# Six product jobs of a two-layer model kernel moved to later steps of its recurrence block, and sixty-five constant products taken out

## The chip, the cores and the metric

The kernel runs on one core of one Trainium2 chip. The metric is device time in microseconds (us), the median over the runs shown. The core's engines are TensorE (PE in the profile; its weight loads are the rows PEld), VectorE (DVE), ScalarE (ACT), GpSimd (POOL) and SyncE (SP), which issues the loads. Each engine takes its own instructions in order, and the engines wait for each other on semaphores.

## The reference, cut to what matters

The model is a stack of two transformer layers with local, low-rank and grouped attention, and then a third layer of another kind. That one has a mixer with four branches (a gated linear recurrence, the gated delta rule, stick-breaking attention and gated linear attention), and a mixture of experts behind it. Sequence 256, model width 1024, all in float32. The change lies in the mixer, where the first two branches are computed:

```python
proj = jnp.einsum("bsd,de->bse", x, w_in)          # one wide input projection for all branches
(a_in, gdn_qkv, gdn_beta_in, gdn_decay_in, gdn_gate_in,
 sb_qkv, gla_qkv, gla_lr, gla_gate_in, merge_in) = jnp.split(proj, offsets, axis=-1)
y_a = rg_lru(a_in, ...)                            # conv, two gates, a scan over time
qkv = silu(causal_depthwise_conv(gdn_qkv, gdn_conv_w))
q = l2_normalize(q) * GDN_DK ** -0.5;  k = l2_normalize(k)
o_b = gated_delta_rule_chunked(q, k, v, g, beta)
y_b = rms_norm_2(o_b, gdn_norm_w) * silu(gdn_gate_in)

def gated_delta_rule_chunked(q, k, v, g, beta):    # chunks of 64, 4 heads of 128
    gc = jnp.cumsum(g, axis=-1)
    decay = jnp.exp(jnp.where(causal, gc[..., :, None] - gc[..., None, :], -jnp.inf))
    a_mat = jnp.where(strict, (k_beta @ k^T) * decay, 0.0)
    t_inv = triangular_solve(a_mat, eye, unit_diagonal=True)
    u = t_inv @ (v * beta);  w = t_inv @ (k_beta * exp(gc))
    attn = (q @ k^T) * decay
    # scan over the 4 chunks:
    v_new = u_i - w_i @ state
    o_i = q_i @ state + attn_i @ v_new
    state = state * gl_i + kd_i^T @ v_new
```

## The kernel before, in words

Every float32 product with a large weight is made of three products of rounded halves. A weight unit of 128 x 2048 numbers (1 MB) is loaded, ACT rounds it to its high half (`Ring.hi`, L166 to L176), DVE subtracts to get the low half (`Ring.lo`, L179 to L188), and TensorE multiplies high by high, high by low and low by high (`products`, L472). The ring of this part holds four raw units and two split pairs: the high half of a unit waits until the unit two before it has been multiplied (`used`), and SyncE issues the load of a unit when the unit four before it has been split (`feed`).

`lru_and_gdn` (L2973) computes the first two branches. They are a chain of small operations that depend on each other, so the rest of the input projection is woven in: 44 jobs, numbered 0 to 43 here, two of them to a unit. Each is 24 products of 128 x 256, ended by one copy out of the bank by ACT (L618, L2823 with silu for jobs 20 to 23, or L2833), into banks 6 and 7 in turn, so a job waits until the job two before it has been copied out. `woven` (L2740) sets the order of all engines from the list `jobs_at`, which says how many jobs follow each of the 44 steps (0 to 43) of the chain. For each step,

- TensorE does its part of the chain's step, then that step's jobs;
- ACT rounds units up to the one after that of the last job so far, then does its part of the chain, then copies the step's jobs out;
- DVE does its part of the chain, then splits units up to the same one.

```python
def unit_after(step, end):
    return split_after.get(step, ring.ahead(beside.jobs[end - 1].unit, 1) if end else first)
```

So the place of a job in the list sets three queues: TensorE's, where ACT rounds the unit ahead and copies out, and where DVE splits.

The chain's steps that matter here: 10, convolution and scan (L3309); 12, squares of q and k (L3315, L3316) behind ACT's silu (L3177, step 11); 13, their sums on TensorE (L3059), then Ln and Exp on ACT (L3184, L3187); 14, q and k scaled (L3321); 15 and 16, the spread decay (L3323, L3324) and its sums on TensorE (L3064, L3065 and sixteen at L3035); 17, the product of k with k (`kks`); 18, of k with q (`qks`), and the masks (L3338 to L3341); 19, the masked products (L3345, L3348); 20, the transpose of one of them (`turns`, L3041) and six mask operations (L3350 to L3357); 21 to 30, five rounds that double the blocks of the triangular inverse (L3035 on TensorE, L3147 on ACT, L3362 to L3372 on DVE); 31, k and v transposed and scaled (L3378, L3210); 32, the products `w_sum` and `uu_sum`; 33 to 40, the scan over four chunks, two steps each (L3119, L3391, L3125 to L3131, L3397); 41 and 42, the output norm (L3147, L3404, L3140, L3224, L3225, L3408).

Where TensorE would wait, the kernel has constant products: `keep_busy` (L266) multiplies the identity by a table of constants into a bank that is free, and nobody reads it. `Beside.keep_busy` (L601) takes the bank that the next job will use. One such product is two MATMUL records in the profile.

Of the kernel before, what the change touches and what calls it, by code (L numbers as in the profile page):

```python
# [229 lines left out]
def program(nc, A, OUT):  # L230
    es = ExitStack()
    with es:
# [2507 lines left out]
        def woven(ring, beside, jobs_at, chains, split_after=()):  # L2740


            ends = list(itertools.accumulate(jobs_at))
            split_after = dict(split_after)
            assert ends[-1] == len(beside.jobs)
            first, last = beside.jobs[0].unit, beside.jobs[-1].unit

            def unit_after(step, end):
                return split_after.get(step, ring.ahead(beside.jobs[end - 1].unit, 1) if end else first)

            with nc.Block() as block:
                @block.sync
                def _(sp):
                    ring.feed(sp, ring.ahead(last, 1))

                @block.tensor
                def _(pe):
                    chain = chains["tensor"](pe)
                    for n in jobs_at:
                        next(chain, None)  # L2760
                        beside.multiply(pe, n)
                    for _ in chain:
                        pass

                @block.scalar
                def _(act):
                    chain = chains["scalar"](act)
                    for step, end in enumerate(ends):
                        ring.hi(act, unit_after(step, end))
                        next(chain, None)  # L2770
                        beside.leave(act, True, end)
                    for _ in chain:
                        pass

                @block.vector
                def _(dve):
                    chain = chains["vector"](dve)
                    for step, end in enumerate(ends):
                        next(chain, None)
                        ring.lo(dve, unit_after(step, end))  # L2780
                        beside.leave(dve, False, end)
                    for _ in chain:
                        pass


        def mixer(ring, s1, U_A, U_QKV, U_GGATE, U_MERGE, U_SB, U_GLA, U_LGATE, U_BR, U_OUT, load_rows):
# [50 lines left out]
            with ExitStack() as s2:  # L2837
# [51 lines left out]
                def small_products(pe):  # L2889
# [3 lines left out]
                    for t in range(TILES):  # L2893
# [3 lines left out]
                        for c in range(KD if t == 0 else 0):  # L2897
# [10 lines left out]
                jobs += fm_jobs(U_GGATE, yT[1], 0, ACT.Silu) + fm_jobs(U_SB[1], sk, all_act=True) + tok_jobs(U_SB[2], sv)  # L2908
                jobs += fm_jobs(U_GLA[0], q, all_act=True) + fm_jobs(U_GLA[1], k, all_act=True) + tok_jobs(U_GLA[2], vt)
                lru_and_gdn(ring, Beside("rec", ring, jobs, (6, 7)), ain, qkv, work, par, w_ax, tok8, hrow, eps_col,  # L2910
                            yT[0], yT[1], (CONV_A, CONV_B, B_A, B_X, LAM, CONV_G, GDN_N))

# [60 lines left out]
        def lru_and_gdn(ring, beside, ain, qkv, work, par, w_ax, tok8, hrow, eps_col, y_lru, y_gdn, columns):  # L2973
# [3 lines left out]
            def W(i):  # L2977
                return work[i]
# [7 lines left out]
            def half(flat, b):  # L2986
                return flat[:, 512 * b:512 * b + 512]
# [10 lines left out]
            with ExitStack() as st:  # L2998
# [27 lines left out]
                def tensor(pe):  # L3026
# [6 lines left out]
                    def eights(banks, left, right, sem):  # L3033
                        for g in range(8):
                            ins = nc.tensor.matmul(ps[banks[g // 4]][:, (g % 4) * P:(g % 4 + 1) * P], left(g), right(g),  # L3035
                                                   start=True, stop=True)
                        ins.then_inc(sem, 1)
# [6 lines left out]
                    def of(i):  # L3044
                        return lambda g: g8(W(i))[:, g, :]
# [31 lines left out]
                    eights((0, 1), lambda g: g8(kT)[:, g, :], lambda g: g8(qT)[:, g, :], qks)  # L3077
                    yield
                    yield
                    beside.keep_busy(pe, 11)  # L3080
                    pe.wait_ge(attn.sem, 2)
                    turns((2, 3), W(AT), an_turned)
                    yield
                    for n in range(5):
                        if n == 0:
                            beside.keep_busy(pe, 31)
                            pe.wait_ge(started.sem, 4)
                            pe.wait_ge(attn.sem, 4)
                        else:
                            pe.wait_ge(u_ready.sem, 2 * n)  # L3090
                        pe.wait_ge(mid_ready.sem, n + 1)
                        eights((0, 1), of(AM), of(U), y_sum)
                        yield
                        pe.wait_ge(y_out.sem, 2 * n + 2)
                        if n:
                            pe.wait_ge(t_ready.sem, 2 * n)
                        eights((2, 3), of(TN), of(Y), u_sum)
                        if n < 4:
                            eights((4, 5), of(Y), of(TN), t_sum)
                        yield  # L3100
# [2 lines left out]
                    turns((0, 1), kT, kv_turned)  # L3103
                    turns((2, 3), vT, kv_turned)
                    yield
                    beside.keep_busy(pe, 8)
                    pe.wait_ge(keyed.sem, 4)
                    eights((4, 5), of(KBE), of(U), w_sum)
                    pe.wait_ge(v_out.sem, 8)
# [23 lines left out]
                        ins.then_inc(o_sum, 1)  # L3133
                        yield
                    yield
                    beside.keep_busy(pe, 7)
                    pe.wait_ge(squared.sem, 3)
                    pe.wait_ge(u_out.sem, 2)
                    for b in range(2):
                        nc.tensor.matmul(ps[b][:, :], ones, half(W(SQ), b), start=True, stop=True).then_inc(n_sum, 1)  # L3140
                    beside.keep_busy(pe, 14)
                    yield

                def scalar(act):
# [263 lines left out]
                    done(dve, v.tensor_tensor(y, y, W(RS), ALU.mult), normed)  # L3408
                    yield

                jobs_at = [2] * 15 + [1, 1, 2, 1, 1] + [0] + [0, 1] * 4 + [0, 0] + [0, 0] + [1, 0] * 4 + [0] * 3
                woven(ring, beside, jobs_at, {"tensor": tensor, "scalar": scalar, "vector": vector})


# [331 lines left out]
```

## Time and profile before

| | us |
|---|---|
| runs shown: median of 3 | 1769.69 |
| lowest and highest | 1764.97, 1770.83 |
| profiled execution, its own time | 1771.72 |
| its span in the trace | 1770.0 |
| PE, DVE, ACT busy over the span | 1646.3, 1222.2, 818.0 |
| mean granted TensorE clock | 0.974 of full speed |

The span is from the first to the last instruction; the rest of the profiled execution's time lies around it. A granted clock of 1.00 is TensorE's upper level, 2.4 GHz, and 0.5 is the lower, 1.2 GHz. Busy time of TensorE counts a MATMUL as busy until its modelled end, so neighbouring rows overlap; the start times tell the pace. The recurrence block lies from about 978 us to 1217 us of the span.

### The profile page before, as it was taken

To read this page: it belongs to the slowest core of one execution; us is meant where nothing else is said; L and a number is where in the kernel's file an instruction comes from. 1 tells how busy PE (TensorE), PEld (TensorE's weight loads), DVE (VectorE), ACT (ScalarE), POOL (GpSimd) and SP (SyncE) were. 2 spreads that over 40 slices of the span, in tenths; PEclk is the share of its full clock that TensorE was granted. 3 is DMA by queue.
4 is the path that set the end of the run, shared out by engine and by line. 5 is a ranking of instruction groups with operands and counts; after the bars stand their busy time and mean duration, and the time that the engine had idled before them with its cause. 6 is when DMAs were issued, how large, how long until landed. Compare 5 with 4: busy or idle time off the path is not lost. (4 is left out here: it accounts for less than half of the span.)

```text
span 1770.0 us, 26752 instructions
## 1 busy us (share of the span) xinstructions
PE 1646.3 (93%) x11331; PEld 1501.3 (85%) x11331; DVE 1222.2 (69%) x1352; ACT 818.0 (46%) x952; POOL 42.9 (2%) x60
## 2 busy tenths in 40 slices
PE   3899998899999999899989899898899999999995
PEld 3889888899898988899979899888888787888884
DVE  5877577888766648756555785633574868899895
ACT  2345543333344554444433465224452347777774
POOL 0100000000010000000000000000000000000000
PEclk9999999999999999999999999998997999999998
DMA  8974435999855324566626564111222447999993
GB/s 306 328 237 151 159 119 159 346 321 323 288 165 153 120 96 128 196 211 215 225 76 192 158 185 126 52 45 48 72 96 72 143 144 249 387 357 367 363 360 127
DMA packets 226061, 348.13 MB, mean 197 GB/s; under 512 B 14612, under 2 KB 156672, under 8 KB 225808
## 3 DMA queue, kind: packets, MB, share of 16 engines
q1 hardware_dynamic: 225936, 346.36, 58.6%
q8 instruction: 91, 1.49, 0.3%
q14 instruction: 34, 0.28, 0.0%
HBM read 345.29 MB, written 1.97 MB: 196 GB/s over the span
## 5 line engine op out<-in xcount | busy, mean ns | idle before, releaser
L472 PE MATMUL bank<-layer_split,hT_pair 128*128 128x256 f32 (+2 forms) x4032 | 515.4, 288 | 19.0 <-DVE hT_pair L1056 7.8
L472 PEld LDWEIGHTS bank<-layer_split,hT_pair 128*128 128x128 f32 x4032 | 488.6, 191 | 32.8 <-issue 15.6
L188 DVE TENSOR_TENSOR layer_split<-layer_raw,layer_split 128x2048 fp32r<-128x2048 f32 x122 | 279.6, 2292 | 100.2 <-ACT layer_split L176 98.7
L176 ACT ACTIVATE layer_split<-layer_raw 128x2048 fp32r<-128x2048 f32 x122 | 233.6, 1915 | 193.8 <-PE bank L472 76.3
L188 DVE TENSOR_TENSOR expert_split<-expert_raw,expert_split 128x2048 fp32r<-128x2048 f32 x96 | 219.0, 2288 | 26.4 <-ACT expert_split L176 26.0
L176 ACT ACTIVATE expert_split<-expert_raw 128x2048 fp32r<-128x2048 f32 x96 | 183.4, 1917 | 55.8 <-PE bank L2515 31.4
L472 PE MATMUL bank<-split_w,hT_pair 128*128 128x256 f32 (+1 forms) x1248 | 175.2, 303 | 12.0 <-ACT mixer_arena L2833 3.6
L472 PEld LDWEIGHTS bank<-split_w,hT_pair 128*128 128x128 f32 x1248 | 164.1, 202 | 22.3 <-issue 12.7
L1931 PE MATMUL bank<-layer_split,ffnh_aT 128*128 128x512 f32 x528 | 127.0, 396 | 2.8 <-DVE ffnh_aT L2005 2.8
L188 DVE TENSOR_TENSOR split_w<-raw_w,split_w 128x2048 fp32r<-128x2048 f32 x39 | 89.4, 2292 | 45.6 <-ACT split_w L176 45.2
L472 PE MATMUL bank<-hT_pair,split_w 128*128 128x256 f32 x960 | 118.5, 283 | 2.0 <-DVE hT_pair L326 1.2
L1931 PEld LDWEIGHTS bank<-layer_split,ffnh_aT 128*128 128x128 f32 x528 | 98.0, 188 | 25.8 <-DVE ffnh_aT L2005 3.3
L472 PEld LDWEIGHTS bank<-hT_pair,split_w 128*128 128x128 f32 x960 | 115.4, 190 | 4.0 <-DVE hT_pair L326 1.8
L176 ACT ACTIVATE split_w<-raw_w 128x2048 fp32r<-128x2048 f32 x39 | 74.6, 1912 | 37.8 <-PE bank L472 33.7
L2515 PE MATMUL bank<-expert_split,hT_pair 128*128 128x512 f32 x384 | 90.4, 392 | 0.9 <-ACT gathered_pair L2626 0.9
L2515 PE MATMUL bank<-expert_split,gathered_pair 128*128 128x512 f32 x384 | 90.7, 392 | 0.0
L266 PE MATMUL bank<-cst 128*128 128x128 f32 x630 | 81.5, 289 | 4.2 <-PEq L3715 4.2
L2515 PEld LDWEIGHTS bank<-expert_split,hT_pair 128*128 128x128 f32 x384 | 71.5, 188 | 16.1 <-ACT gathered_pair L2626 1.3
L2515 PEld LDWEIGHTS bank<-expert_split,gathered_pair 128*128 128x128 f32 x384 | 71.5, 188 | 14.8
L266 PEld LDWEIGHTS bank<-cst 128*128 128x128 f32 x630 | 78.2, 203 | 5.4 <-issue 5.1
L1972 ACT ACTIVATE ffnh_aT<-bank 128x512 fp32r<-128x512 f32 x22 | 13.1, 597 | 85.9 <-PE bank L1919 85.9
L208 DVE SCALAR_TENSOR_TENSOR ada_acc<-layer_raw,silu_c,ada_acc 128x1024 f32<-128x1024 f32 x40 | 51.4, 1285 | 1.4
(470 smaller groups left out, 1966.4 us busy)
## 6 DMA issues: line engine op xcount, KB each, us to landing
layer_raw<-in_ada_w SPq DMA_DIRECT2D x48, 1024.0 KB, 7.1
layer_raw<-in_ffn_w_gate_up SPq DMA_DIRECT2D x44, 1024.0 KB, 6.1
layer_raw<-in_w_in SPq DMA_DIRECT2D x38, 1024.0 KB, 6.6
expert_raw<-in_w_gate SPq DMA_DIRECT2D x32, 1024.0 KB, 7.5
expert_raw<-in_w_up SPq DMA_DIRECT2D x32, 1024.0 KB, 7.5
expert_raw<-in_w_down SPq DMA_DIRECT2D x32, 1024.0 KB, 7.4
raw_w<-in_w_in SPq DMA_DIRECT2D x30, 1024.0 KB, 5.5
layer_raw<-in_ffn_w_down SPq DMA_DIRECT2D x22, 1024.0 KB, 5.6
```

The source lines that it names most:

```text
L176: self.nc.scalar.activation(self.pair[:, j % self.pairs, 0, 0:self.size[n]], self.raw[n % self.depth][:, 0:self.size[n]], ACT.Copy).then_i ...
L188: self.nc.vector.tensor_tensor(self.pair[:, j % self.pairs, 1, 0:self.size[n]], self.raw[n % self.depth][:, 0:self.size[n]], self.pair[:, ...
L208: self.nc.vector.scalar_tensor_tensor(acc[:, :], second, self.scale[:, 2 * q + 1:2 * q + 2], acc[:, :], ALU.mult, ALU.add).then_inc(self.l ...
L266: nc.tensor.matmul(ps[bank][:, 0:P], ident, cst[:, 0:P], start=True, stop=True)
L472: ins = nc.tensor.matmul(out, lhs, rhs, start=first and c == chunks[0] and tp + wp == 0, stop=last and c == chunks[-1] and tp == 1)
L1931: ins = nc.tensor.matmul(ps[4 + 2 * t + nb][:, :], self.aT[:, tp, c, t * P:(t + 1) * P], w[:, c, nb * 512:(nb + 1) * 512], start=n == 0 an ...
L1972: nc.scalar.activation(self.aT[:, 0, :, :].rearrange(flat), ps[2][:, :], ACT.Copy).then_inc(self.hi_out, 1)
L2515: ins = nc.tensor.matmul(ps[bank][:, :], gathered[e // PER // 2][:, tp, 4 * i + c, slot_cut(e // PER)], ring.view(u + i, wp, 4, 512)[:, c, :],
```

## The change

Nothing is computed otherwise. The list `jobs_at` has the same 44 steps and the same sum; jobs leave steps 10 to 14 (one of two in each) and step 16, and are put behind steps 19 (one more), 20 (two), 32, 41 and 42 (one each). By the cumulative count the step of every job from 21 on is another than before, steps 22 to 28 and 33 to 39 keep one job at every other step. Constant products: all 11 ahead of the transpose in step 20, 25 of 31 in step 21, all 8 in step 32, all 7 and all 14 in step 42 are taken out. The 6 left in step 21 and the 4 in step 31 stay.

```diff
@@ -3077,13 +3077,12 @@
                     yield
                     yield
-                    beside.keep_busy(pe, 11)
                     pe.wait_ge(attn.sem, 2)
                     turns((2, 3), W(AT), an_turned)
                     yield
                     for n in range(5):
                         if n == 0:
-                            beside.keep_busy(pe, 31)
+                            beside.keep_busy(pe, 6)
                             pe.wait_ge(started.sem, 4)
                             pe.wait_ge(attn.sem, 4)
@@ -3103,7 +3102,6 @@
                     turns((0, 1), kT, kv_turned)
                     turns((2, 3), vT, kv_turned)
                     yield
-                    beside.keep_busy(pe, 8)
                     pe.wait_ge(keyed.sem, 4)
                     eights((4, 5), of(KBE), of(U), w_sum)
@@ -3133,12 +3131,10 @@
                         yield
                     yield
-                    beside.keep_busy(pe, 7)
                     pe.wait_ge(squared.sem, 3)
                     pe.wait_ge(u_out.sem, 2)
                     for b in range(2):
                         nc.tensor.matmul(ps[b][:, :], ones, half(W(SQ), b), start=True, stop=True).then_inc(n_sum, 1)
-                    beside.keep_busy(pe, 14)
                     yield
@@ -3408,7 +3404,7 @@
-                jobs_at = [2] * 15 + [1, 1, 2, 1, 1] + [0] + [0, 1] * 4 + [0, 0] + [0, 0] + [1, 0] * 4 + [0] * 3
+                jobs_at = [2] * 10 + [1] * 5 + [1, 0, 2, 1, 2] + [2] + [0, 1] * 4 + [0, 0] + [0, 1] + [1, 0] * 4 + [1, 1, 0]
                 woven(ring, beside, jobs_at, {"tensor": tensor, "scalar": scalar, "vector": vector})
```

## Rows read from the trace of the kernel before

**Rows 1.** Stages of the block: busy us and count of each engine, granted clock, DMA share, GB/s.

```profile
1035.00:1065.00 30.00, 29.15 (x246) 28.64 (x245) 24.96 (x27) 19.11 (x21) 0.00 (x0) 1.00 0.57 176
1065.00:1083.50 18.50, 17.47 (x131) 15.38 (x129) 8.57 (x7) 14.43 (x16) 0.00 (x0) 1.00 0.52 158
...
1118.20:1163.60 45.40, 38.80 (x328) 37.66 (x328) 23.10 (x26) 10.56 (x16) 0.00 (x0) 1.00 0.16 47
...
1171.50:1206.40 34.90, 34.90 (x226) 30.72 (x224) 10.61 (x18) 6.22 (x8) 0.00 (x0) 0.90 0.20 61
1206.40:1217.30 10.90, 8.38 (x48) 7.15 (x47) 3.74 (x3) 6.08 (x7) 0.00 (x0) 0.82 0.00 0
```

**Rows 2.** Timeline, steps 9 to 18: start, length, engine, line, what, [idle before, releaser].

```profile
1042.06 23.06 PE L472 MATMUL bank<-hT_pair,split_w 128*128 128x256 f32 x192 [0.39 <-DVE split_w L188]
...
1050.23 1.28 ACT L2823 ACT_TABLE_LOAD   x1
1051.20 2.29 DVE L188 TENSOR_TENSOR split_w<-raw_w,split_w 128x2048 fp32r<-128x2048 f32 x1
1051.52 0.38 ACT L2823 ACTIVATE y_gdn<-bank 128x256 f32<-128x256 f32 x1
...
1055.76 2.94 ACT L3177 ACTIVATE mixer_arena<-mixer_arena 128x1024 f32<-128x1024 f32 x3
...
1058.74 1.23 DVE L3315 TENSOR_TENSOR mixer_arena<-mixer_arena 128x1024 f32<-128x1024 f32 x1 [0.55 <-ACT mixer_arena L3177]
...
1064.96 3.59 PE L3059 MATMUL bank<-mixer_arena,cst 128*128 128x512 f32 x8
...
1068.65 2.85 ACT L3184 ACTIVATE mixer_arena<-bank,eps_column 128x512 f32<-128x512 f32 x4
...
1072.81 2.00 ACT L3187 ACTIVATE mixer_arena<-mixer_arena 128x1024 f32<-128x1024 f32 x2
1073.90 2.49 DVE L3321 SCALAR_TENSOR_TENSOR mixer_arena<-mixer_arena 128x1024 f32<-128x1024 f32 x2 [4.24 <-ACT mixer_arena L3187]
...
1075.25 1.92 ACT L176 ACTIVATE split_w<-raw_w 128x2048 fp32r<-128x2048 f32 x1
...
1079.48 0.69 DVE L3323 COPY mixer_arena<-gdn_tok 128x1024 f32<-128x1024 f32 x1
...
1083.50 0.28 PE L3064 MATMUL bank<-gdn_tok,cst_second 128*128 128x8 f32 x2
...
1087.43 2.99 PE L472 MATMUL bank<-split_w,hT_pair 128*128 128x256 f32 x24
...
1097.70 1.95 PE L3035 MATMUL bank<-mixer_arena 128*128 128x128 f32 x16
```

**Rows 3.** Timeline, steps 19 to 21: the mask phase.

```profile
1107.63 1.40 DVE L3345 TENSOR_TENSOR mixer_arena<-mixer_arena,bank 128x512 f32<-128x512 f32 x2
...
1109.08 1.09 PE L3041 MATMUL bank<-cst,mixer_arena 128*128 128x128 f32 x8 [1.33 <-DVE mixer_arena L3345]
...
1110.01 7.09 PE L266 MATMUL bank<-cst 128*128 128x128 f32 x62
1110.50 1.22 DVE L3350 TENSOR_TENSOR mixer_arena<-mixer_arena,cst_second 128x1024 f32<-128x1024 f32 x1
...
1118.27 2.05 PE L3035 MATMUL bank<-mixer_arena 128*128 128x128 f32 x16 [1.17 <-DVE mixer_arena L3357]
```

**Rows 4.** Timeline, steps 32 and 33.

```profile
1167.77 3.84 PE L3035 MATMUL bank<-mixer_arena 128*128 128x128 f32 x32 [0.37 <-DVE mixer_arena L3378]
...
1171.54 1.09 PE L3119 MATMUL bank<-mixer_arena 128*64 128x128 f32 x8
```

**Rows 5.** Timeline, steps 41 and 42: the tail.

```profile
1206.47 3.35 PE L266 MATMUL bank<-cst 128*128 128x128 f32 x14
...
1210.83 0.69 ACT L3224 ACTIVATE mixer_arena<-bank,eps_column 128x512 f32<-128x512 f32 x1 [1.87 <-PE bank L3140]
...
1211.49 3.29 PE L266 MATMUL bank<-cst 128*128 128x128 f32 x28
```

## The prediction

> **What bounds the kernel now.** I read the page for the busy shares, then the table of stages of the block that is changed, then its timeline row by row. In the stages before the mask phase TensorE is busy 29.15 of 30.0 us and 17.47 of 18.5 us, with DVE at 24.96 and 8.57 [rows 1]. The reader should see the pace: eight jobs run without a break in 23.06 us, 2.88 us each [rows 2]. So TensorE sets the pace there, with DVE and ACT not far behind. In the mask phase it is the other way round: the 62 constant records stand inside DVE's six mask operations, and the next product waited for DVE, not for TensorE [rows 3]. In the inverse rounds one job a round lies on TensorE's path; that stays. The granted clock is 1.00 up to the inverse and falls to 0.90 and 0.82 in the scan and the tail [rows 1].
>
> **The change: 1. Six jobs leave steps 10 to 16.** If TensorE alone set the pace they would give 6 x 2.88 = 17.3 us. I follow the chain with one job a step. Jobs 18 to 22 end at 1042.06 + 5 x 2.88 = 1056.5. ACT has the silu table at 1050.23 + 1.28, copies job 20 out (0.38) and can start the silu (2.94 us) at 1051.9 instead of 1055.76, as the scan's operations and their split start at 1051.20 and the convolution is over before; it ends at 1054.9. The two squares (about 1.26 each from L3315's 1.23) end at 1057.4, and TensorE's sums (3.59 us) run from 1056.5 to 1060.1 [rows 2].
>
> ACT meanwhile rounds unit 12 (1.92), copies job 22 out and loads the table of Ln: ready at 1058.8. Ln 2.85, table 1.28, Exp 2.00 take it to 1065.0, and q and k are scaled at 1066.5 (L3321 ends 3.58 us after L3187 begins). Now comes something new: job 23 is a silu job and its copy lands behind the Exp. It needs the silu table again, 1.28 + 0.38 = 1066.6, and only then unit 13 is rounded (1068.5) and split (2.29: 1070.8), ahead of the spread decay on DVE (0.69: 1071.5). TensorE's L3064 starts at 1071.6 instead of 1083.50: 11.9 us earlier [rows 2]. TensorE has done jobs 24 and 25 by then, and waits some 2 us. From L3064 to the product of k with q it is 14.20 us before, with three jobs in it; two are left, one 2.88 less. Total of this part: **-14.8 us**. The Exp table has to come back too, in step 17, but there its result is asked for only after two more jobs, 5.8 us of TensorE. Bounds: -17.3 if nothing of ACT or DVE shows; -9.3 if one more round of table load, rounding and split (1.28 + 1.92 + 2.29 = 5.5) falls into the chain than I counted.
>
> What the chain of steps 10 to 16 is worth hangs on the table load. The row shows 1.28 us and the next activation 0.01 us behind it [rows 2]. The Trainium skill, "ScalarE: Activation LUTs", section "What ACT_TABLE_LOAD costs", gives about 1.28 us for the load and about 1.38 us more for a drain at each switch; with the drain at the three switches in the chain this part would be about 4 us smaller by an estimate from that page. The row shows no such drain, so the sum goes without it.
>
> **2. The mask phase.** Steps 19 and 20 get three jobs more (8.6 us of TensorE at 2.88), for 36 constant products of about 0.23 us (7.09 / 31), 8.2 us [rows 3]. That exchange is even and lies beside DVE's masks. But each engine's queue moves with the jobs. Step 18's split (now of unit 15, before of unit 18) stays where it was, in front of L3345. Unit 16 must now be split behind the masked products of step 19, ahead of L3350 on DVE's queue, and nothing stood between L3348 and L3350 before: 2.29 us on the path to the inverse's first product. ACT can round it in time, since job 29, which frees the pair, ends some 5 us before. Job 30 waits for unit 15's split, so TensorE stands idle some 2.5 us there, and the transpose starts about 1.6 us after its time of 1109.08; DVE needs it two masks after L3350, some 4 us later. Unit 17's split falls behind the last mask, beside the first product (2.05 us), and is hidden [rows 3]. **+2.3 us**; bounds 0, if ACT's wait covers it, and +4.6, if both splits show.
>
> **3. Inverse rounds.** One job in every second step as before. The splits move from rounds 1 and 3 to rounds 2 and 4, and DVE has 23.10 busy of 45.4 us there [rows 1]: nothing.
>
> **4. Step 32.** Eight constant products stood ahead of the wait for the scaled keys; they were free. The job 37 stands behind the 32 records of L3035, and the scan's first product L3119 started at 1171.54, 3.77 us after they started, right behind them [rows 4]. Everything in the scan hangs on that product, and each of its steps has a job as before. So the job's whole 2.9 us are on the path: **+2.9 us**. Bounds: 0, and +4.6 if it runs at the lower clock (below).
>
> **5. The tail.** Job 42 takes the place of the 7 constant products and of the rest of the wait for the squares: 1206.47 + 2.9 = 1209.4, just when the sums could start. But ACT now copies it out (0.38) before it loads the Ln table (1.28), which was loaded in idle time: L3224 starts at 1211.1 instead of 1210.83, say 0.4 with the hand-overs. And in this very place the 14 records took 3.35 us where 28 took 3.29 us later [rows 5]: lower clock, 1.2 GHz, behind the scan's short products. A job there loses 3.35 / 2 = 1.7 us. I take it: **+2.1 us**, bounds 0 and 2.1. Job 43 replaces the last 28 records (3.29 by 2.88) and hides behind Ln, Exp and the last product; unit 22's split moves behind the squares on DVE, where DVE waits for ACT's Ln and Exp in any case.
>
> **Loads.** SyncE's next loads follow the splits, some up to 20 us later than before. The DMA share is 0.57 and less [rows 1], and a unit is taken only every 3 to 10 us; four raw units stand ahead. No cost.
>
> **Sum**: -14.8 + 2.3 + 2.9 + 2.1 = **-7.5 us**. The profiled execution takes 1771.72 us, its span 1770.0; they would become 1764.2 and 1762.5. It stands 2.0 us above the median of the runs shown, 1769.69, so the median would be **1762.2 us**.
>
> **The rivals.**
>
> *The lead gives less.* ACT and DVE have 19.11 and 24.96 of 30 us [rows 1], and ACT's waits are taken away with the jobs. With the bound of -9.3 the sum is -2.0: 1767.7 us. Against it: the chain above counts each of their operations already. Chance 0.25.
>
> *The clock falls where the constant products went.* It is 0.90 in the scan [rows 1], and was at the lower level in the tail, right behind the scan's short products [rows 5]. In steps 31 and 32 only the transposes of k and v and the wait for the scaled keys are left between the inverse and L3035 x32. If it falls there, those 3.84 us [rows 4] lose up to 1.7 us: -5.8, 1763.9 us. Chance 0.12. In the mask phase a fall would be hidden: TensorE has some 3 us to spare. By the Trainium skill, "TensorE: Matmul & The Clock Gate", section "Part 4: PE-mode transpose", transposes do not count as activity for the clock, which speaks for this rival; rows 4 and 5 show no stretch of transposes with nothing else around them, so the trace is silent.
>
> *The lead gives nearly all.* The silu job's table load is hidden and the tail keeps the upper clock: -17.3 + 2.3 + 2.9 + 0.4 = -11.7, 1758.0 us. Chance 0.10.
>
> *Slower.* TensorE is busy in the lead only because its jobs fill a wait; what sets the end of step 16 is the chain silu, squares, Ln, Exp, scaling, spread on ACT and DVE, and its start hangs on the splits that DVE makes one behind the other. DVE's 24.96 of 30 us speaks for it. Then part 1 gives nothing and the added 2.3 + 2.9 + 2.1 = 7.3 stay: 1777.0 us. It decides from where part 1 gives under 2.0 us. Against it: the silu could have started 3.9 us earlier but for jobs 21 to 23 and their copies [rows 2], and TensorE's run of 23.06 us has no hole. Chance 0.08.
>
> **How the numbers follow.** The forecast, with 5.3 to 11 us saved, has 0.45. A difference under 0.3% (5.3 us) can't be told from none here: the three runs lie 5.9 us apart. Faster: 0.45 + 0.10 + half of the clock's 0.12 = 0.61. Within: 0.25 + 0.06 = 0.31. Slower: 0.08. The range goes from a little below the better case to just past the smaller lead, 1757 to 1769.5 us, and leaves the slower case out.
>
> **What would show it.** In the trace of the changed kernel: L3064 some 12 us and the product of k with q some 14 to 15 us earlier, and an added table load for L2823 and for L3193; a split L188 between L3348 and L3350, so that from L3345 to the inverse's first product 13 us pass and not 10.6; a job L472 x24 between L3035 x32 and the first L3119; job 42 from the end of the scan to the norm's sums, at 2.9 or 4.6 us. The forecast is wrong if the block's end comes less than 5 us earlier, or if the stages outside the block move.

## The result, and the profile after

The changed kernel takes **1757.51 us** (median of 10 runs, 1750.87 to 1762.47) against 1769.31 us for the kernel before in the same comparison (10 runs, 1762.95 to 1776.68): ratio 0.992, 95% interval 0.9903 to 0.9937, or 14.2 us less, with 11 to 17 in the interval (the ratio is taken over all runs; the medians themselves lie 11.8 us apart). The profiled execution takes 1758.45 us (span 1756.8) against 1771.72. Faster by more than 0.3% came true; the forecast of 1762.2 us took little over half of the gain. A second comparison (e10, below) gave 0.9935, and both together are about -12 us.

The totals of the page say little: TensorE's busy share stays at 93%.

```profile
span 1756.8 us, 26496 instructions
PE 1626.4 (93%) x11201; PEld 1483.1 (84%) x11201; DVE 1222.2 (70%) x1352; ACT 820.5 (47%) x954; POOL 46.5 (3%) x60
```

The stages of the block, in the changed kernel (columns as in [rows 1]):

```profile
1036.50:1066.50 30.00, 29.36 (x225) 26.93 (x224) 23.97 (x28) 24.17 (x27) 0.00 (x0) 1.00 0.57 176
1066.50:1072.60 6.10, 3.80 (x30) 3.39 (x29) 4.03 (x4) 4.97 (x6) 0.00 (x0) 1.00 0.01 3
1119.90:1159.60 39.70, 32.25 (x274) 31.06 (x272) 21.10 (x24) 11.51 (x22) 0.00 (x0) 1.00 0.18 54
1168.00:1203.00 35.00, 35.00 (x225) 30.77 (x225) 10.69 (x18) 7.32 (x8) 0.00 (x0) 0.90 0.20 61
1203.00:1213.90 10.90, 7.43 (x53) 6.27 (x52) 6.03 (x4) 6.74 (x9) 0.00 (x0) 1.00 0.31 96
```

ACT went from 19.11 to 24.17 us in the first 30, DVE stayed near 24, and then come 6.1 us in which TensorE has work for 3.80: at that point the pace has passed from TensorE to ACT and DVE. The tail kept the upper clock, 1.00 where it was 0.82.

Timeline of the lead in the changed kernel, from the sums of squares to the first products behind the spread decay:

```profile
1057.96 3.60 PE L3059 MATMUL bank<-mixer_arena,cst 128*128 128x512 f32 x8
...
1064.05 2.01 ACT L3183 ACTIVATE mixer_arena<-mixer_arena 128x1024 f32<-128x1024 f32 x2
1066.07 1.28 ACT L2823 ACT_TABLE_LOAD   x1
1067.37 0.38 ACT L2823 ACTIVATE y_gdn<-bank 128x256 f32<-128x256 f32 x1
1067.65 1.90 ACT L176 ACTIVATE split_w<-raw_w 128x2048 fp32r<-128x2048 f32 x1
1069.65 2.29 DVE L188 TENSOR_TENSOR split_w<-raw_w,split_w 128x2048 fp32r<-128x2048 f32 x1 [2.04 <-ACT split_w L176]
1071.86 0.69 DVE L3319 COPY mixer_arena<-gdn_tok 128x1024 f32<-128x1024 f32 x1
1072.60 0.39 PE L3064 MATMUL bank<-gdn_tok,cst_second 128*128 128x8 f32 x2 [1.70 <-DVE mixer_arena L3319]
```

Read down this list as one chain: Exp, the silu table loaded again for job 23, its copy, the rounding of a unit, its split, the spread, and only then TensorE. Six of the eight rows are ACT and DVE. The mask phase of the same kernel:

```profile
1095.73 1.40 DVE L3341 TENSOR_TENSOR mixer_arena<-mixer_arena,bank 128x512 f32<-128x512 f32 x2
1095.87 3.10 PE L472 MATMUL bank<-split_w,hT_pair 128*128 128x256 f32 x24 [2.66 <-DVE split_w L188]
1098.61 2.29 DVE L188 TENSOR_TENSOR split_w<-first_unit_raw,split_w 128x2048 fp32r<-128x2048 f32 x1
1100.82 1.22 DVE L3346 TENSOR_TENSOR mixer_arena<-mixer_arena,cst_second 128x1024 f32<-128x1024 f32 x1
...
1108.57 3.68 PE L3035 MATMUL bank<-mixer_arena 128*128 128x128 f32 x16 [1.94 <-DVE mixer_arena L3353]
```

A split of 2.29 us stands between the masked products and the next mask, where in [rows 3] nothing stood, and the job of step 19 waited 2.66 us for its split. Steps 31 to 33 and the tail of the same kernel:

```profile
1159.68 5.47 PE L3035 MATMUL bank<-mixer_arena 128*128 128x128 f32 x32 [2.16 <-DVE mixer_arena L3374]
1164.91 3.07 PE L472 MATMUL bank<-hT_pair,split_w 128*128 128x256 f32 x24
1167.91 1.09 PE L3117 MATMUL bank<-mixer_arena 128*64 128x128 f32 x8
...
1202.97 3.00 PE L472 MATMUL bank<-split_w,hT_pair 128*128 128x256 f32 x24
1206.41 1.28 ACT L3220 ACT_TABLE_LOAD   x1
1207.71 1.41 ACT L3220 ACTIVATE mixer_arena<-bank,eps_column 128x512 f32<-128x512 f32 x2
```

The job stands whole between the 32 records and the scan's first product. The records themselves took 5.47 us where [rows 4] has 3.84.

### The profile page after: what moved, and what is told of

The parts are those of the page before. It is cut to its first block and busy times, and to the rows that moved or that the text cites. A ratio compares the mean times of both kernels' runs of the same rounds, so it can differ in the third digit from the quotient of the medians.

```text
span 1756.8 us, 26496 instructions
## 1 busy us (share of the span) xinstructions
PE 1626.4 (93%) x11201; PEld 1483.1 (84%) x11201; DVE 1222.2 (70%) x1352; ACT 820.5 (47%) x954; POOL 46.5 (3%) x60
## 5 line engine op out<-in xcount | busy, mean ns | idle before, releaser
L472 PE MATMUL bank<-split_w,hT_pair 128*128 128x256 f32 (+1 forms) x1248 | 169.1, 296 | 13.3 <-PEq L513 3.5
L472 PEld LDWEIGHTS bank<-split_w,hT_pair 128*128 128x128 f32 x1248 | 158.1, 195 | 22.9 <-issue 11.4
L2515 PEld LDWEIGHTS bank<-expert_split,gathered_pair 128*128 128x128 f32 x384 | 71.5, 188 | 14.8
L266 PE MATMUL bank<-cst 128*128 128x128 f32 x500 | 67.1, 295 | 4.2 <-PEq L3711 4.2
L266 PEld LDWEIGHTS bank<-cst 128*128 128x128 f32 x500 | 64.4, 209 | 4.9 <-issue 4.7
```

The lines of the kernel that those rows point to most:

```text
L266: nc.tensor.matmul(ps[bank][:, 0:P], ident, cst[:, 0:P], start=True, stop=True)
L472: ins = nc.tensor.matmul(out, lhs, rhs, start=first and c == chunks[0] and tp + wp == 0, stop=last and c == chunks[-1] and tp == 1)
L2515: ins = nc.tensor.matmul(ps[bank][:, :], gathered[e // PER // 2][:, tp, 4 * i + c, slot_cut(e // PER)], ring.view(u + i, wp, 4, 512)[:, c, :],
```

## The experiments

Two questions stand behind them. Does each part of the change give what the forecast said, or did one (the lead above all) give more (e1 to e4, e6 to e8, e11, e12)? And is the rest of the gain the change's at all, or the comparison's, the clock's, or that of a mere shift of later stages (e5, e9, e10, e13 to e16)?

Line numbers in the diffs' kernels lie up to four below those of before. "Block" is the time from the table load of the first square root (1037.75 us in the kernel before; "after the square root" below counts from there too) to stick-breaking's first product, in one profile. The "lead" is the part up to the first masked product. Times are medians; "mean" is said where a mean is meant.

**e1: the lead and the mask phase in part.** Three jobs leave the lead, three enter steps 19 and 20.

```diff
-                    beside.keep_busy(pe, 11)
-                            beside.keep_busy(pe, 31)
+                            beside.keep_busy(pe, 6)
-jobs_at = [2] * 15 + [1, 1, 2, 1, 1] + [0] + [0, 1] * 4 + [0, 0] + [0, 0] + [1, 0] * 4 + [0] * 3
+jobs_at = [2] * 10 + [1] * 3 + [2] * 2 + [1, 1, 2, 1, 2] + [2] + [0, 1] * 4 + [0, 0] + [0, 0] + [1, 0] * 4 + [0] * 3
```

> Kernel before with three jobs taken from steps 10, 11, 12 and put behind steps 19 (one) and 20 (two), 36 constant products of the mask phase out, the rest (8, 7, 14) kept. Theory A (all gain is TensorE time taken from the lead, part by part, the clock is chance): three jobs give 3 x 2.88 = 8.6 us, the split between the masked products and the masks costs 2.2: -6.4 us, near 1763 us; from the first masked product to the first product of the inverse 12.8 us pass. Theory B (the change also acts on the stage of the gated linear attention, 100 us later, through the clock): 9 to 16 us saved, and that stage's scan is at the upper clock in this profile too.

1765.99 us (12 runs), ratio 0.9983 (0.9962 to 1.0003), before 1769.79. The timeline of the step behind the silu job:

```profile
1076.31 10.04 PE L472 MATMUL bank<-hT_pair,split_w 128*128 128x256 f32 x72 [8.41 <-ACT y_gdn L2823]
```

TensorE waited 8.41 us for the copy of job 23, which stands behind the Exp on ACT. The lead gave only 1.9 us for three jobs, and the mask phase cost its 2.2 us. Near 1763 us, 6.4 less, was expected; 3.8 less came, and the interval reaches from 0.9962 to past 1, so even that isn't clear. Which jobs leave matters as much as how many.

**e2: the other half.** Three jobs leave the lead, one goes to step 32 and two to the tail.

```diff
-                    beside.keep_busy(pe, 8)
-                    beside.keep_busy(pe, 7)
-                    beside.keep_busy(pe, 14)
-jobs_at = [2] * 15 + [1, 1, 2, 1, 1] + [0] + [0, 1] * 4 + [0, 0] + [0, 0] + [1, 0] * 4 + [0] * 3
+jobs_at = [2] * 13 + [1] * 2 + [1, 0, 2, 1, 1] + [0] + [0, 1] * 4 + [0, 0] + [0, 1] + [1, 0] * 4 + [1, 1, 0]
```

> Kernel before with three jobs taken from steps 13, 14, 16 and put behind steps 32, 41, 42, the constant products 8, 7, 14 out, those of the mask phase (11 and 31) kept. Theory A: 8.6 us from the lead, 2.9 given back in step 32, 0.4 in the tail: -5.3 us, near 1764 us; the first product of the scan starts 6.6 us behind the start of the 32 records before it at the upper clock, 8.2 at the lower one. Theory B: 8 to 15 us saved.

1760.02 us (8 runs), 0.9946 (0.9922 to 0.9969). The lead gave 12.0 us for three jobs, more than the 8.6 that they take on TensorE. The timeline of DVE shows where the rest comes from:

```profile
1083.80 2.29 DVE L188 TENSOR_TENSOR split_w<-first_unit_raw,split_w 128x2048 fp32r<-128x2048 f32 x1 [6.09 <-ACT split_w L176]
...
1089.36 1.23 DVE L3338 TENSOR_TENSOR mixer_arena<-mixer_arena,cst_second 128x1024 f32<-128x1024 f32 x1
1090.62 1.41 DVE L3342 TENSOR_TENSOR mixer_arena<-mixer_arena,bank 128x512 f32<-128x512 f32 x2
...
1093.50 2.29 DVE L188 TENSOR_TENSOR split_w<-raw_w,split_w 128x2048 fp32r<-128x2048 f32 x1
1095.71 1.22 DVE L3347 TENSOR_TENSOR mixer_arena<-mixer_arena,cst_second 128x1024 f32<-128x1024 f32 x1
```

A unit feeds two jobs, so its rounding and split fall in every second job. With an odd number of jobs ahead, step 18 has neither, and the masks of step 18 follow each other without a gap. But the split isn't gone: it stands behind the masked products now (1093.50), and from the first of them to the inverse's first product 12.85 us pass, where the kernel before has 10.64 with the same jobs and constants in that phase. So parity gave up to 3.4 us in the lead and took 2.2 back, about 1.2 us net. The whole time fell by 9.6 us where 5.3 were expected.

**e3: the job of step 32 in step 31**, ahead of L3035 x32 and beside DVE's last work on the inverse; otherwise the changed kernel.

```diff
-... + [0, 0] + [0, 1] + [1, 0] * 4 + [1, 1, 0]
+... + [0, 0] + [1, 0] + [1, 0] * 4 + [1, 1, 0]
```

> Changed kernel with the job of step 32 one step earlier, behind the transposes of k and v and ahead of the wait for the scaled keys. Theory A: the job runs in a wait of 2.4 us and costs 0.5 us where it cost 2.9: 2.4 us less than the changed kernel, and no low clock in the 32 records behind it (another 0 to 1.6): near 1754 us. Rival: the job was hidden in the wait for w and u behind step 32 already; then no difference.

1753.33 us (6 runs), 0.9918 (0.9889 to 0.9946).

```profile
1151.71 3.08 PE L472 MATMUL bank<-hT_pair,split_w 128*128 128x256 f32 x24
1154.63 3.73 PE L3035 MATMUL bank<-mixer_arena 128*128 128x128 f32 x32
1158.29 1.09 PE L3117 MATMUL bank<-mixer_arena 128*64 128x128 f32 x8
```

The scan's first product follows the 32 records directly again. From DVE's first L3364 in the inverse rounds (L3368 before) to it 48.17 us pass, 2.4 less than with the job in between at the upper clock (50.6): the price of step 32 is the job itself. Near 1754 us was expected.

**e4: the constants of step 32 back**, beside the job.

```diff
+                    beside.keep_busy(pe, 8)
                     pe.wait_ge(keyed.sem, 4)
```

> Changed kernel with the eight constant products ahead of the wait for the scaled keys put back. Theory A: they fill a wait and cost nothing; they keep the upper clock over the 32 records behind them, which took 5.47 us in the changed kernel and 3.84 in the kernel before: 0 to 1.6 us less than the changed kernel, mean 0.8. Rival (the low clock there is chance, not the missing products): the records can be at either clock here too, no difference on average.

1755.66 us (7 runs), 0.9927 (0.99 to 0.9954).

```profile
1156.68 1.95 PE L266 MATMUL bank<-cst 128*128 128x128 f32 x16
1159.01 3.84 PE L3035 MATMUL bank<-mixer_arena 128*128 128x128 f32 x32 [0.37 <-DVE mixer_arena L3375]
...
1165.60 1.09 PE L3118 MATMUL bank<-mixer_arena 128*64 128x128 f32 x8
```

The 32 records run at the upper clock, 3.84 us. Over all profiles without these constants and with the job behind the 32 records (the changed kernel twice, e2, e6, e7) they took 5.46 or 5.47 us in three and 3.84 in two. With something in the wait they never fell: 3.84 us in all eight profiles with the eight constants (this one and seven of kernels that kept them and have no job there), 3.73 in all five with a job there (e3, e8, e11, e12, e16). The Trainium skill, "TensorE: Matmul & The Clock Gate", section "Part 4: PE-mode transpose", has transposes not count as activity for the clock; the three falls of five, behind transposes and a wait of 2.16 us, agree with it. But the transposes stand in all eighteen profiles, so what these runs show is that the unfilled wait makes the difference, and not that transposes do.

**e5: the kernel before once more**, one run with a profile, no edit.

> The kernel before, a second profile. In the first one the stages behind the block (first stick-breaking product to the end) took 552.6 us, in the profiles of the changed kernel and the four variants 542.8 to 550.5. Theory A (where the clock falls there is chance): they take 543 to 552 us here too, and the block, from ACT's square root to the first stick-breaking product, 179.7 us again, give or take 1.7 us for a low stretch. Theory B (the change acts on the later stages): 552 us or more.

1767.03 us, span 1765.27. Its block takes 178.64 us against 179.66 in the profile ahead of the prediction, so that block repeats within 1.5 us (178.22 in e9), while its span is 4.7 us less. The difference lies in other stages.

**e6: the split held back.** Unit 13 (jobs 26 and 27) is rounded and split behind the spread decay on DVE, not ahead of it.

```diff
-woven(ring, beside, jobs_at, {"tensor": tensor, "scalar": scalar, "vector": vector})
+woven(ring, beside, jobs_at, {"tensor": tensor, "scalar": scalar, "vector": vector}, split_after={14: ring.ahead(beside.jobs[23].unit, 1)})
```

> Changed kernel, with the rounding and split of unit 13 held from step 14 to step 15, behind the spread decay. Theory: the chain of steps 10 to 16 hangs on ACT's two table loads and this split, not on TensorE: the spread decay starts right behind the scaling, about 4 us earlier, then TensorE's job 25 (which waits for the silu copy) is the last to come: L3064 1.8 us earlier than in the changed kernel (33.4 us behind the square root's start becomes 31.6), the whole time 1.8 us less. Rival (TensorE's jobs set the end of this part): no difference.

1754.52 us (6 runs), 0.9917 (0.9891 to 0.9942).

```profile
1064.41 0.69 DVE L3319 COPY mixer_arena<-gdn_tok 128x1024 f32<-128x1024 f32 x1
1064.56 3.09 PE L472 MATMUL bank<-hT_pair,split_w 128*128 128x256 f32 x24 [0.59 <-ACT y_gdn L2823]
...
1066.69 2.29 DVE L188 TENSOR_TENSOR split_w<-raw_w,split_w 128x2048 fp32r<-128x2048 f32 x1 [0.86 <-ACT split_w L176]
1067.49 0.28 PE L3064 MATMUL bank<-gdn_tok,cst_second 128*128 128x8 f32 x2
```

The spread runs ahead of the split, and L3064 comes 31.52 us after the square root instead of 33.38: 1.9 us of the lead had hung on DVE's order. What comes last ahead of L3064 now is job 25 on TensorE, which waits for the silu copy. So the chain that the prediction followed is the real one there.

**e7: the split of the mask phase held back**, with a job of step 20 moved to step 30.

```diff
-... [1, 0, 2, 1, 2] + [2] + [0, 1] * 4 + [0, 0] + [0, 1] + ...
+... [1, 0, 2, 1, 2] + [1] + [0, 1] * 4 + [0, 1] + [0, 1] + ...
+ split_after={19: ring.ahead(beside.jobs[29].unit, 1)}
```

> Changed kernel with one of the two jobs of step 20 moved to step 30, the last inverse round, and the split of unit 16 held from step 19 to step 20, behind the masks. Theory: the 2.3 us between the masked products and the masks go: from L3341 to the first inverse product 10.6 us and not 12.8; the job in round 5 costs 1.2 us, as 1.7 of its 2.9 us fill a wait: in all 1.0 us less than the changed kernel. Rival (TensorE was late for the masks in any case): 12.8 us stay and the sum is 1.2 us more.

1759.34 us (6 runs), 0.9937 (0.9913 to 0.9962).

```profile
1092.05 1.40 DVE L3341 TENSOR_TENSOR mixer_arena<-mixer_arena,bank 128x512 f32<-128x512 f32 x2
...
1094.92 1.22 DVE L3346 TENSOR_TENSOR mixer_arena<-mixer_arena,cst_second 128x1024 f32<-128x1024 f32 x1
...
1102.69 2.05 PE L3035 MATMUL bank<-mixer_arena 128*128 128x128 f32 x16 [2.46 <-DVE mixer_arena L3353]
```

From the first row to the last 10.64 us pass, as before the change [rows 3], and not 12.84: the split was the whole added cost of the mask phase. But the job in step 30 cost 2.0 us, where 1.2 were expected, and took it back: the mean is 0.5 us above the changed kernel's 1757.6, where 1.0 less was expected.

**e8: both holds and step 31 together.**

```diff
-... [1, 0, 2, 1, 2] + [2] + [0, 1] * 4 + [0, 0] + [0, 1] + ...
+... [1, 0, 2, 1, 2] + [1] + [0, 1] * 4 + [0, 1] + [1, 0] + ...
+ split_after={14: ring.ahead(beside.jobs[23].unit, 1), 19: ring.ahead(beside.jobs[29].unit, 1)}
```

> Changed kernel with the job of step 32 in step 31, the held split of unit 13, and one job of step 20 in step 30 with the held split of unit 16. If the parts add: 2.4 to 4 + 1.8 + 1.0 = 5 to 7 us less than the changed kernel, near 1751 us. Rival (a part only fills a wait that another opens): 3 us or less.

1753.98 us (6 runs), 0.9907 (0.988 to 0.9934); block 166.4 us, 12.5 less than the mean of before (178.8). The mean is 3.8 us less than the changed kernel's, where 5 to 7 were expected.

**e9 and e10: the kernel before against itself, and the changed kernel again**, no edits. They ask whether a comparison favours the kernel that is run second, and whether the first -14.2 us repeat.

> The kernel before, unchanged, timed as a variant. Every variant so far, whichever jobs it moves, came out some 3 us faster than its stages in the profile account for at the upper clock. Theory A: the comparison is fair and the rest is low-clock time that the change saves: this one comes out within 1.5 us of the kernel before (1769 to 1771). Rival (a variant gains some 3 us only by its place in the comparison): 1766 to 1767.

> The changed kernel, unchanged, with more runs and a second profile. Theory A: 13 us less than the kernel before, as in the ten runs so far; its block, from ACT's square root to the first stick-breaking product, takes 170 us and 1.6 for each low stretch that meets TensorE's path, 170 to 175; the kernel before has 178.6 and 179.7 in its two profiles. Rival (the first ten runs were lucky with the clock): 9 to 10 us less.

e9: 1768.5 us (12 runs), 0.9994 (0.9977 to 1.0011); no favour for the second place is seen, but the interval has room for one of up to 4 us. e10: 1758.35 us (10 runs), 0.9935 (0.9913 to 0.9958). With the first ten the changed kernel has a mean of 1757.6 us; the kernel before has 1769.85 over the 83 runs of the four later comparisons. That is -12.2, with about 2 us either way.

**e11: an odd number of jobs ahead of step 17**, with e6's hold and the step moved as in e3.

```diff
-jobs_at = [2] * 10 + [1] * 5 + [1, 0, 2, 1, 2] + [2] + [0, 1] * 4 + [0, 0] + [0, 1] + [1, 0] * 4 + [1, 1, 0]
+jobs_at = [2] * 10 + [1] * 5 + [0, 0, 2, 1, 2] + [2] + [0, 1] * 4 + [0, 1] + [1, 0] + [1, 0] * 4 + [1, 1, 0]
+ split_after={14: ring.ahead(beside.jobs[23].unit, 1)}
```

> Changed kernel with no job behind step 15 (so jobs 25 and 26, of different units, stand behind step 17), one more behind step 30, the job of step 32 in step 31, and unit 13's split held to step 15. Theory (what the mask phase waits for is the rounding of the next unit, which waits for the second job of a unit): with a job's shift no unit is rounded or split in step 18; from L3064 to the first masked product 17.6 us as in the variant with the end part alone, not 21.4 at the upper clock; L3064 2.4 us earlier again. Lead 8 us shorter than in the changed kernel, steps 30 to 32 1 us shorter: 9 us less in all, near 1748 us. Rival (TensorE's work sets the mask phase's start): 3 us less.

**1750.35 us** (6 runs, 1747.54 to 1753.73), 0.9895 (0.9871 to 0.9918), the lowest median of all. Near 1748 was expected.

```profile
1064.56 0.39 PE L3064 MATMUL bank<-gdn_tok,cst_second 128*128 128x8 f32 x2 [1.19 <-DVE mixer_arena L3319]
...
1073.73 1.92 ACT L176 ACTIVATE split_w<-raw_w 128x2048 fp32r<-128x2048 f32 x1 [7.76 <-PE bank L472]
...
1078.10 2.05 PE L3035 MATMUL bank<-mixer_arena 128*128 128x128 f32 x16 [1.64 <-ACT mixer_arena L3189]
...
1082.67 1.22 DVE L3337 TENSOR_TENSOR mixer_arena<-mixer_arena,cst_second 128x1024 f32<-128x1024 f32 x1
1083.92 1.41 DVE L3341 TENSOR_TENSOR mixer_arena<-mixer_arena,bank 128x512 f32<-128x512 f32 x2
```

L3064 comes 29.2 us after the square root, 2.3 us ahead of e6, and the masks are unbroken. From L3064 to the last row it took 19.36 us, not the 17.6 expected: ACT's rounding of step 17 waited until 1073.73 for the end of job 25 and held L3189 back, and TensorE waited 1.64 us for it. The mask phase behind keeps its 12.85 us. Against e6 the first masked product comes 4.4 us earlier with one job less ahead of it (2.9), so the parity gave about 1.5.

**e12: e3 with e6's hold.**

> Changed kernel with the job of step 32 in step 31 and unit 13's split held to step 15. Both parts were seen alone: 2.4 and 1.9 us. If they add: 4.3 us less than the changed kernel, near 1752.5 us; block of 165.7 us at the upper clock.

1755.0 us (6 runs), 0.9912 (0.9885 to 0.9939), before 1769.66, where 1752.5 was expected; block 167.1. The hold's 1.9 us can't be seen in the whole time beside e3 (both medians lie in each other's spread); in the block the two are alike because e12 took 39.5 us from the scan's first product to the norm's sums, and e3 38.1.

**e13, e14, e15: a shift alone.** Theory C in the expectations says: what the block doesn't explain comes from the later stages starting at another time. The kernel before, with 4, 8 or 12 constant products ahead of stick-breaking's first, which delays all that follows. **e16** is e11 with 4.

```diff
+                    keep_busy(5, 4)
                     for i in range(PAIRS + 2):
```

> Kernel before with 4 constant products (0.9 us) ahead of the first product of stick-breaking, behind the block. Theory C (where the clock falls depends on when a stage starts, so a shift alone changes the time): the gated linear attention's scan has 10 us at the lower clock, not 20 to 31, and the time falls by 2 to 5 us although 0.9 us of work is added. Chance: 0.9 us more than the kernel before, the scan at 10 to 31 us of lower clock as it falls.

> Kernel before with 8 constant products (1.8 us) in the same place. Theory C: 1 to 3 us less than the kernel before, the scan's lower clock at 10 to 14 us. Chance: 1.8 us more.

> Kernel before with 12 constant products (2.8 us) in the same place. Theory C: the three kernels do not lie on a line of 0.9, 1.8, 2.8 us; this one within 2 us of the kernel before, or above. Chance: 2.8 us more.

> The variant with the shifted jobs (no job behind step 15) with 4 constant products ahead of stick-breaking. Its scan had 20 us at the lower clock. Theory C: 10 us there, 2 to 4 us less than that variant's 1750.4. Chance: 0.9 us more.

1769.34 us (0.9996, 0.9979 to 1.0013), 1769.81 (1.0018, 1.0002 to 1.0035) and 1772.87 (1.0028, 1.001 to 1.0047), 12 runs each; e16 1754.05 (8 runs), 0.9932 (0.9908 to 0.9955). The means are 0.0, +1.7 and +3.2 us above the 31 runs of before in that comparison, for 0.9, 1.8 and 2.8 us of products at the upper clock. They rise with the work that was added: no delay of 1 to 3 us gains anything by itself, and theory C falls for shifts of that size. The changed kernels start what follows the block up to 14 us earlier by their blocks, and no run tests a shift of that size or in that direction. e16 came out 3.7 us above e11 for 0.9 us of added work, so e11's 1750.35 was in part luck: the two together, less the 0.9, have a mean of 1752.5, within 2 us of e3, e6 and e8.

## Why the prediction was right in its steps and wrong in its size

**Part 1, the lead: right.** From the square root to L3341 (before: L3345) it was 69.88, 70.18 and 69.88 us in the three profiles of before, 54.88 in those of the changed kernel (e10) and of e3 and e4, and 56.51 in the changed kernel's first, where a stretch at 1.2 GHz around 1075 us cost 1.6. That is -15.0, or -14.3 over the two profiles, for -14.8 forecast; the product of k with q, which the forecast named, came 15.0 us earlier in e10. L3064 came 12.4 us earlier for 11.9. The table load for the silu job, its 0.01 to 0.02 us to the next activation, and the split ahead of the spread stand in the timeline as the chain had them.

**The mask phase: right.** 12.84 us for 10.64 up to the inverse's product chain, +2.2 for +2.3; e7 took exactly this away. TensorE's wait was 2.66 for some 2.5.

**Step 32: right, with the rival inside it.** 50.6 us for 47.88 at the upper clock, +2.7 for +2.9; e3 took 2.4 of it away. In three of five profiles the 32 records fell to the lower clock and cost 1.6 more. That rival had 0.12; it was true more often than not.

**The tail: a little too dear.** The forecast took the lower clock for job 42, 4.6 us, and +2.1 in sum. The job took 3.00 us in the changed kernel's first profile, e6 and e7, and 4.4 to 4.6 in e10 and seven others. From the scan's first product to the tail's last operation (L3408) the mean is 42.9 us over six profiles without the jobs and 44.3 over ten with them, +1.4. With the scan itself at the same pace, it is 43.6 for 43.4 where job 42 had the upper level (+0.2) and 45.2 for 43.4 where it had the lower (+1.8; e8, e11, e12).

So the parts add up to -15.0 + 2.2 + 2.7 + 0.2 = -9.9 us where the upper clock holds. With the losses at the lower clock in (the tail's mean, and three fifths of 1.6 in step 32) it is -15.0 + 2.2 + 2.7 + 1.4 + 1.0 = -7.7. The block of the changed kernel fell by 4.0 us in its first profile, which had two more stretches at the lower clock, and by 7.3 in e10. The forecast was -7.5: for the block it was good. But the whole time fell by 12.2.

**The step that failed** is the one that set the sum of the block equal to the change of the whole: the -7.5 us were taken off one profiled execution ("The profiled execution takes 1771.72 us, its span 1770.0; they would become 1764.2 and 1762.5") and off the median, and everything outside the block was put at nothing. The prediction named its own sign of that, "if the stages outside the block move", and by the whole times they did: 12.2 us against a block that fell by 5.7 in the mean of two profiles. How whole and block stand to each other, for every kernel with moved jobs and, below the line, for those without (change of the mean of the timed runs against 1769.85; change of the block against 178.8, one profile each, two for the changed kernel):

```
kernel    whole   block
e1         -3.4    +1.1
e2         -9.4    -4.4
changed   -12.2    -5.7
e4        -12.9    -7.6
e7        -11.8    -7.6
e3        -15.6   -11.3
e6        -15.8   -11.1
e8        -16.0   -12.5
e12       -14.5   -11.7
e11       -19.3   -14.1
e16       -15.0   -14.4
--
e9         -1.4    -0.6
e13        -0.8    +2.9
e14        +1.0    +4.4
e15        +2.5    +3.8
```

The order is nearly the same, so the block tells roughly which version is better. But the whole is 2.8 to 6.5 us further down in the first ten kernels and 0.6 in e16, 4.2 in the mean of all eleven. The four without the change show some of it too: with their constants taken out of both times, 1.6 in the mean. Part of this is found. The granted clock is not the same in all runs: over 222 timed runs of all kernels, those of one kernel differ with a standard deviation of 3.8 us, and the time rises by 0.31 us with each microsecond at the lower level (correlation 0.86; time at the lower level worked out from each run's mean clock). The 83 runs of before had 84.9 us at that level in the mean, the 20 of the changed kernel 79.1 (74.8 in the first ten, 83.4 in e10). At equal clock the change is -10.4 and not -12.2 by this estimate, and the first comparison, at -14.2, was lucky by some 2 us. Whether the change itself saves time at the lower level or only drew it, these runs can't tell. For the eleven kernels the same step takes 1.4 us of the 4.2, for the four others 1.0 of the 1.6.

A stage that the change doesn't touch shows how much the clock can do: the gated linear attention's scan, the same instructions, 50 us each from 0.5 us ahead of it. The kernel before, e5 (the same kernel), and the changed kernel:

```profile
1313.00:1363.00 50.00, 48.81 (x325) 45.78 (x318) 32.00 (x68) 12.02 (x15) 0.00 (x0) 0.73 0.22 73
```

```profile
1313.60:1363.60 50.00, 49.13 (x335) 44.81 (x328) 32.80 (x68) 13.92 (x18) 0.00 (x0) 0.80 0.26 85
```

```profile
1307.80:1357.80 50.00, 49.14 (x355) 44.09 (x348) 35.11 (x71) 16.15 (x20) 0.00 (x0) 0.90 0.26 85
```

The granted clock is 0.73, 0.80 and 0.90, and TensorE gets through 325, 335 and 355 records in the same 50 us. Two rounds of the scan (from the second to the fourth run of DVE's L3690) took 31.8, 27.1 and 22.3 us, with 20.1, 10.2 and 0.0 us of them at the lower level. It isn't the change that makes it: e10 is the changed kernel at 0.80, and e15, the kernel before with a delay, had 0.90:

```profile
1304.30:1354.30 50.00, 49.14 (x335) 44.84 (x328) 32.75 (x68) 13.92 (x18) 0.00 (x0) 0.80 0.25 85
```

```profile
1315.30:1365.30 50.00, 49.14 (x354) 44.23 (x348) 35.00 (x71) 16.01 (x20) 0.00 (x0) 0.90 0.25 85
```

Of the 13.2 us between the spans of the two profiled executions, 4.9 are the block's and 9.8 lie behind it (the changed kernel started its block 1.5 later), and this scan alone makes 9.5: a reader who compares only these two would credit the change with a draw of the clock.

**What stays open**: about 3 us, at equal clock, by which the changed kernels in the mean gained more than their block, where the four others gained some 0.5. e9 doesn't show it as the place in a comparison, but could not exclude that; a later start of 1 to 3 us doesn't give it (e13 to e15), an earlier one wasn't tested. The profiles don't show it: the time ahead of the block differs by 0.6 us between six profiles of before and its delayed versions and twelve of the others, and that behind stick-breaking's start by 0.5, with single profiles 5 us and more off either way. No run here isolated it, and its cause stays open.

The median of 1757.51 lies only 0.5 us inside the range. Set against the kernel before in the same comparison it lies outside: the ratio is 0.992, and the range ended at 1757 / 1769.69 = 0.9928. It is near the case "the lead gives nearly all" (1758.0), but not by that case: the lead gave what the forecast said, and the rest came from outside the block. The mis-sized terms inside it are the tail, +2.1 for a measured +1.4, and step 32's clock, 1.0 in the mean, left out of the likeliest case; they nearly cancel.

## What to carry to other kernels

Moving filler work into waits moves what each queue does for it as well: its rounding, split, copy and table load. Count these one by one, and look at the parity of shared units, which here was worth 1.2 to 1.5 us net, about half a job (e2, e11); a side operation held back by one place on its queue took its whole cost out of a stage, 1.9 and 2.2 us here (e6, e7). Before a block's sum is set against the whole time, take two or three profiles of the kernel before and see how much the untouched stages move by themselves.

## What was not expected of the hardware

- The same short-product scan took 22.3 to 31.8 us by the granted clock: in all eighteen profiles its length less half of its time at the lower level is 21.1 to 22.5. The runs of the kernel before lie 10 to 16 us apart in a comparison, mostly by the clock (correlation 0.86).
- A wait of 2.16 us behind transposes was followed by 32 records partly at the lower level in three of five profiles (5.47 us for 3.84), and in none of the thirteen in which constants or a job stood in that wait.
- An extra table load costs its 1.28 us and no more: the next activation stands 0.02 us behind it in the changed kernel's lead. The drain of about 1.38 us that the Trainium skill, "ScalarE: Activation LUTs", section "What ACT_TABLE_LOAD costs", adds to each switch is not seen in any of these rows, so the measurement decides.
